# Up projection from the unscaled residual stream, with the norm's factor per token multiplied in by GpSimd

## The reference

```python
h = h + rmsnorm(mix, g_mix_post[i])
u = rmsnorm(h, g_ffn_pre[i])
up = causal_depthwise_conv(u @ w_up[i], conv_w[i], conv_b[i])
gate_ff, value = jnp.split(up, [D_FF], axis=-1)
f = (jax.nn.gelu(gate_ff, approximate=True) * value) @ w_down[i]
h = h + rmsnorm(f, g_ffn_post[i])
```

## Time and profile before

| | us |
|---|---|
| median of 3 runs | 3159.44 |
| lowest, highest | 3158.5, 3162.44 |
| profiled execution, its own time | 3159.64 |
| its span in the profile | 3157.8 |
| PE busy | 3089.1 |
| DVE busy | 1969.8 |
| ACT busy | 1419.3 |
| POOL busy | 35.0 |

### The profile page before, as it was taken

How to read it: one execution, slowest core, us unless ns; L and a number is a source line. 1 busy time by engine, 2 the same in 40 slices (tenths; PEclk the granted TensorE clock), 3 DMA queues, 4 the chain that set the end, 5 groups by cost and what they waited for, 6 DMA issues and landing times.

```text
span 3157.8 us, 41441 instructions
## 1 busy us (share of the span) xinstructions
PE 3089.1 (98%) x16976; PEld 2667.6 (84%) x16976; DVE 1969.8 (62%) x2503; ACT 1419.3 (45%) x2026; POOL 35.0 (1%) x30
## 2 busy tenths in 40 slices
PE   8999999989999999999999999999999999999998
PEld 8988887878888888878788888888889999899986
DVE  6767676788888878767867665342743444444444
ACT  5344555455555544436422222233644534544453
POOL 0000002000000000000000000000000000000000
PEclk9999999999999999999999999999999999999999
DMA  8777666756766778775555565343333333333343
GB/s 292 230 244 227 200 207 206 243 173 214 226 215 218 225 232 276 253 241 196 162 181 174 176 203 178 112 151 98 101 97 104 101 107 110 104 107 101 108 147 120
DMA packets 369837, 557.59 MB, mean 177 GB/s; under 512 B 16944, under 2 KB 239152, under 8 KB 368368
## 3 DMA queue, kind: packets, MB, share of 16 engines
q1 hardware_dynamic: 366784, 540.08, 53.4%
q0 software_dynamic: 2000, 12.06, 1.0%
q10 hardware_dynamic: 864, 2.80, 0.2%
HBM read 552.64 MB, written 2.23 MB: 176 GB/s over the span
## 4 chain that ended last, share of the span: by engine, by line
PE 91%; DVE 3%; ACT 2%; DMA 2%; issue 1%; SPq 0%; DVEq 0%; ACTq 0%
PE ps L708 87%; DVE wlo L1680 1%; DMA raw<-in_w_in 1%; ACT whi L1114 1%; PE ps L909 0%; PE ps L924 0%; PE ps L914 0%; PE ps L926 0%; DMA CX<-in_ctx 0%; DVE acc L1697 0%; PE ps L778 0%; PE ps L743 0%; DMA gb_c<-in_g_ffn_post 0%; DVE HCl L1834 0%; PE ps L837 0%
## 5 line engine op out<-in xcount | busy, mean ns | idle before, releaser
L1680 DVE TENSOR_TENSOR wlo<-raw,whi 128x1024 fp32r<-128x1024 f32 (+1 forms) x823 | 1002.1, 1223 | 827.6 <-ACT whi L1114 825.7
L1114 ACT ACTIVATE whi<-raw 128x1024 fp32r<-128x1024 f32 x828 | 868.1, 1056 | 1094.7 <-PE ps L708 1070.2
L708 PE MATMUL ps<-HCh,whi 128*128 128x512 f32 (+1 forms) x1816 | 508.1, 361 | 1.0 <-DVE HCl L1834 1.0
L708 PE MATMUL ps<-HCh,wlo 128*128 128x512 f32 (+1 forms) x1816 | 500.7, 357 | 0.0
L708 PE MATMUL ps<-HCl,whi 128*128 128x512 f32 (+1 forms) x1816 | 500.2, 357 | 0.0
L708 PE MATMUL ps<-V,whi 128*128 128x512 f32 x1408 | 444.1, 397 | 0.9 <-DVE V L1836 0.9
L1697 DVE SCALAR_TENSOR_TENSOR acc<-raw_ada,S,acc 128x1024 f32<-128x1024 f32 x330 | 420.8, 1285 | 8.1 <-DMA raw_ada<-in_ada_w 7.9
L708 PEld LDWEIGHTS ps<-HCl,whi 128*128 128x128 f32 x1816 | 323.5, 189 | 49.8
L708 PEld LDWEIGHTS ps<-HCh,wlo 128*128 128x128 f32 x1816 | 323.4, 189 | 49.9
L708 PEld LDWEIGHTS ps<-HCh,whi 128*128 128x128 f32 x1816 | 319.3, 189 | 51.0 <-issue 4.2
L708 PEld LDWEIGHTS ps<-V,wlo 128*128 128x128 f32 x1408 | 264.8, 188 | 62.6
(11 more groups left out here) (341 smaller groups left out, 3419.3 us busy)
## 6 DMA issues: line engine op xcount, KB each, us to landing
raw_ada<-in_ada_w SPq DMA_DIRECT2D x192, 512.0 KB, 4.8
raw<-in_w_up SPq DMA_DIRECT2D x176, 512.0 KB, 4.7
raw<-in_w_in SPq DMA_DIRECT2D x160, 512.0 KB, 3.9
raw<-in_od_w_in SPq DMA_DIRECT2D x160, 512.0 KB, 3.5
raw<-in_ev_w_in SPq DMA_DIRECT2D x96, 512.0 KB, 3.7
raw<-in_w_down SPq DMA_DIRECT2D x88, 512.0 KB, 5.1
raw<-in_w_out SPq DMA_DIRECT2D x32, 512.0 KB, 4.7
raw<-in_w_ple_gate SPq DMA_DIRECT2D x32, 512.0 KB, 4.5
```

The source lines that it names most:

```text
L708: mm = e.matmul(o, a, b, start=first and t == 0, stop=last, skip_group_check=True)
L1114: e.activation(m.whi[ch.i % SPLIT][:, 0:n], m.raw[ch.slot][:, 0:n], ACT.Copy).then_inc(S("hi"), 1)
L1680: e.tensor_tensor(m.wlo[ch.i % SPLIT][:, 0:n], m.raw[ch.slot][:, 0:n], m.whi[ch.i % SPLIT][:, 0:n].bitcast(F32), ALU.subtract).then_inc(S( ...
```

## The change

The up groups no longer take the normalized stream. V is made from `H` itself times `g_ffn_pre`, and PE turns `H` directly: `hnb` and line 1822 are gone for V. A column block is turned as soon as its two `residual` instructions are done. On DVE these alternate with the low parts of V. On ACT the eight squares no longer stand ahead of V; two of them follow each of the first four chunks' splits. The sum, the root and the inverse of norm `nb2` follow as steps beside `up1` and `up2`, then PE turns the factor into a row (`rsd2`, in the tenth chunk of the up stage), and DVE copies it to `rsb2` (128 x 256, the same row in every partition).

GpSimd multiplies `us` by `rsb2` after DVE's addition, 44 instructions of 128x512. ACT's first step of the convolution (line 1441 before, 1481 now) waits for `up_s`, the multiplication, in place of `set`, the addition. For groups 0, 1 and 2, whose factor isn't there in time, the step is put off by 7, 3 and 3 chunks on ACT and DVE (`LATE`). The load of gelu's table is put ahead of the first gelu.

```diff
+LATE = {0: 7, 1: 3, 2: 3}
...
-        self.V = Turned(self, "half", cut(V[:, 0, :, :]), cut(V[:, 1, :, :]), True,
-                        self.sb("hnb", [128, 2, 2, 512], F32, F + 104), None, lambda k: V[:, :, k, :])
+        self.V = Turned(self, "half", cut(V[:, 0, :, :]), cut(V[:, 1, :, :]), False, None, None,
+                        lambda k: V[:, :, k, :])
+        self.V.after = "b"
...
+    e.wait_ge(S("rsb2"), 1)
+    for n in range(2 * NUP):
+        G = plan.by[f"up{n}"]
+        e.wait_ge(S(f"set{G.s}"), G.freed)
+        us = m.us[n % 2]
+        e.tensor_tensor(us[:, :, :], us[:, :, :], m.rsb2[:, :].unsqueeze(1).to_broadcast([128, 2, T]),
+                        ALU.mult).then_inc(S("up_s"), 1)
     e.wait_ge(S("mm"), plan.by[f"up{2 * NUP - 1}"].done)
     e.dma_start(m.gb_c[:, :], A["g_ffn_post"].to_broadcast([128, D])).then_inc(S("ld_gb"), 16)
...
-                e.wait_ge(S("res"), 8 * RESIDUAL["c"] + 2 * (k // 4) + 2)
+                e.wait_ge(S("res"), 8 * RESIDUAL[X.after] + 2 * (k // 4) + 2)
...
-    for n in range(8):
-        P.again(m.nb2, "b", m.H, m.jb, n)
-    P.root(m.nb2)
     V = P.turned(m.V, lambda k: m.v("g_ffn_pre", k))
+
+    def factors():
+        for n in range(8):
+            P.again(m.nb2, "b", m.H, m.jb, n)
+            if n % 2:
+                yield
+        yield
+        yield
+        P.root(m.nb2)
+        P.gelu()
+        yield
+
+    P.beside.append(factors())
+    V.upto(0)
...
-        e.wait_ge(S(f"set{G.s}"), G.freed)
+        for _ in range(LATE.get(n, 0)):
+            yield
+        e.wait_ge(S("up_s"), n + 1)
...
-    residuals("b", m.Yw, m.H, m.nb.rs)
-    P.total(m.nb2)
-    P.invert(m.nb2)
-    V = P.turned(m.V, m.H, m.nb2.rs, lambda k: m.v("g_ffn_pre", k))
+    e.wait_ge(S("yg"), P.n_yg)
+    e.wait_ge(*P.freed)
+    V = P.turned(m.V, None, None, lambda k: m.v("g_ffn_pre", k))
+    for n in range(4):
+        P.residual("b", m.Yw, m.H, m.nb.rs, n)
+    V.upto(1)
+    for n in range(4, 8):
+        P.residual("b", m.Yw, m.H, m.nb.rs, n)
+        V.upto(n - 2)
+
+    def factors():
+        for _ in range(4):
+            yield
+        P.total(m.nb2)
+        yield
+        yield
+        yield
+        P.invert(m.nb2)
+        for b in range(2):
+            t = e.tensor_scalar(m.rsd2[:, b, :], m.ones[:, :], m.nb2.rs[:, b:b + 1], None, ALU.mult)
+        t.then_inc(S("rsd2"), 1)
+        yield
+        yield
+        e.wait_ge(S("rst2"), 1)
+        e.tensor_copy(m.rsb2[:, :], PS[4][:, 0:T]).then_inc(S("rsb2"), 1)
+        yield
```

More of the change, by code:

```diff
@@ L272, in __init__ @@
         self.third = third
+        self.after = "c"
         self.n_p, self.n_n = m.turns.get(row, (0, 0))
@@ L309, in __init__ @@
         at += 2.5
+        self.ji_at = at
         self.ji = self.sb("ji", [128, 2, 512], BF16, at)
@@ L373, in __init__ @@
         V = self.sb("V", [128, 2, NT, T], F32R, F)
-        self.V = Turned(self, "half", cut(V[:, 0, :, :]), cut(V[:, 1, :, :]), True,
-                        self.sb("hnb", [128, 2, 2, 512], F32, F + 104), None, lambda k: V[:, :, k, :])
+        self.V = Turned(self, "half", cut(V[:, 0, :, :]), cut(V[:, 1, :, :]), False, None, None,
+                        lambda k: V[:, :, k, :])
+        self.V.after = "b"
+        self.rsb2 = self.sb("rsb2", [128, T], F32, self.ji_at)
+        self.rsd2 = self.sb("rsd2", [128, 2, 128], F32, self.ji_at + 1)
         self.ACh, self.ACl = self.halves("AC", NF, T, F + 32)
@@ L996, in tensor @@
     X = P.turned(m.V)
+    def factors():
+        for _ in range(9):
+            yield
+        e.wait_ge(S("rsd2"), 1)
+        for b in range(2):
+            t = e.transpose(m.PS[4][:, 128 * b:128 * b + 128], m.rsd2[:, b, :], m.ident)
+        t.then_inc(S("rst2"), 1)
+        yield
+    P.beside.append(factors())
     for g in range(2 * NUP):
@@ L1120, in modulate, with gelu @@
             e.activation(m.R[l][:, :], m.PS[6 + l][:, :], ACT.Copy).then_inc(S("ada_R"), 1)
+    def gelu(self):
+        self.e.activation(self.m.SM[:, 24:25], self.m.ones[:, 0:1], ACT.Gelu_apprx_tanh)
     def warm(self):
```

## The result

| | us |
|---|---|
| changed kernel, median of 4 runs | 3189.12 (3187.57 to 3190.04) |
| kernel before, median of 4 runs on the same chip | 3160.94 (3158.5 to 3162.6) |
| ratio, 95% interval | 1.0087 (1.0074 to 1.0099) |
| span of the profiled execution, before and after | 3157.8 and 3187.9 |

The change makes the kernel 0.9% slower. Of the 30.1 us between the two spans, the timelines place all but a fraction. The first view is PE's timeline of the changed kernel, from the opening to the second stall; it answers to the earlier trace rows.

What follows compares the result with a forecast made beforehand. PE bounds the kernel, busy 3089.1 of 3157.8 us; the change makes DVE the bound in the up groups. Opening -5.3, link +28.7 and stage end +6.3 give +29.7 on 3159.44: 3189 us, range 3174 to 3205.

Steps and rivals of the forecast that it cites:

- The opening: Border of out3 and up0: first product 6.4 us earlier, 1.1 given back for squares, a gain of 5.3 us.
- The link: Up groups: GpSimd's multiplication, 1.25 us plus 0.11 for the step between engines, adds 1.36 us between addition and convolution.
- The bound: Up groups: DVE, with 0.66 us slack, becomes the bound; 0.70 us a group from group 3, 28.7 us lost.
- The period: Up stage: PE's time for a group, read as 11.11 us from 36 groups in a 400 us window.
- One sign: Up stage, changed kernel's trace: PE would have some 40 waits for wlo that sum to 28 us.
- The lock: SBUF exclusion between DVE and GpSimd: priced at nothing from group 3, at most 3.8 us for groups 0 to 2.
- The end of the stage: At down0: gb_c issued after up43's multiplication, 4.1 us more DVE wait plus 2.2 us lost lead, together 6.3 us.
- That the wait is hidden: Up stage: nothing starves, only the opening counts, 3158 us; both hidden cases together had chance 0.10.
- A slower GpSimd: Up stage: multiplication longer than half a wide row, 3204 us at 1.6 us, 3237 at 2.4; chance 0.08.

Runs made afterwards that it cites:

- e3: Changed kernel with ACT's first convolution step and DVE's taps one chunk later in groups 3 to 43 too; 3156.44 us, ratio 0.9990 to the kernel before.
- e1: Changed kernel without GpSimd's 44 multiplications, ACT waiting for DVE's addition again; 3155.71 us, ratio 0.9985 to the kernel before.
- e8: Kernel before with only GpSimd's multiplication (by ones) added between DVE's addition and ACT's first convolution step; 3195.08 us, ratio 1.0110.
- e2: Changed kernel with GpSimd multiplying 128x256 of the 128x512 elements, still one instruction a group; 3166.95 us, ratio 1.0020 to the kernel before.
- e4: Changed kernel with the multiplication done by DVE right behind its addition, GpSimd idle in the stage; 3163.46 us, ratio 1.0009 to the kernel before.
- e6: Kernel before with DVE's wait for gb_c put behind down0's splits; 3157.48 us, ratio 0.9994.
- e7: Changed kernel with steps one chunk later in all groups and the gb_c wait behind down0's splits; 3151.96 us, ratio 0.9975 to the kernel before.
- e5: Changed kernel with DVE's wait for gb_c put behind down0's splits; 3179.34 us, ratio 1.0059 to the kernel before.

## Why the prediction was right

The forecast was 3189; 3189.1 was measured. By its own steps:

- **The opening.** The first transposes were put at 643.3 and started at 643.42; the first product at 645.6, and it started at 645.70. 1.1 us were to be given back for the squares, and 1.4 were, which leaves 4.9 us for a forecast of 5.3. That the two are so close is luck. The squares cost their 0.35 us once, not three times; the other 1.0 us is PE's clock, granted at 0.53 instead of 0.78 in the first 4.3 us of products, for which the prediction had no term.
- **The link.** The multiplication was taken as 1.25 us from half of a wide row plus a fixed part; it takes 1.29 (half of 512 takes 0.737, so the fixed part is nearer 0.18 than 0.10). The link was put at 1.36 and is 1.37.
- **The bound.** DVE's wait was to be 2.59 and is 2.60; its waits for `whi` were to go, and went from 23.9 to 5.1. The loss was put at 28.7 and is 29.1 us. The period was read too short: the window of 400 us doesn't hold 36 whole groups, and from `up1` to `down0` a group took 11.20 us, not 11.11 (and then 11.88, not 11.79); this falls out of the difference. Two smaller errors cancel. PE first stood still five groups behind the start of `up1`, not from group 3 on, so the lead lasted longer; and behind it the loss was 0.74 us a group, not 0.70. One sign wasn't met as written: PE has 22 waits for `wlo` of 20.5 us, not some 40 of 28 us. Of the 29.1 us, 7.3 lie in what the profile counts as busy.
- **The lock.** It was priced at nothing in the changed kernel, since DVE stands still. e3 measured it where DVE doesn't: 0.83 us of DVE a group, against the 1.3 that I had written down for it. The Trainium skill, "SBUF — State Buffer", "Who interferes with whom", says that a DVE instruction with two SBUF inputs contends with a GpSimd instruction that reads SBUF. The trace agrees: the split beside POOL takes 2.32 us instead of 1.22. The prediction took from it that splits between the addition and the taps would lose 1.25 us a group in another way; in e3, which has this order, DVE loses 0.83 and PE nothing.
- **The end of the stage.** The term was 6.3 us and 6.1 were measured, but its parts were wrong. `gb_c` was to land 9.41 us after its issue, as before; it took 7.3. DVE waited 8.72 us, 2.0 more than before and not 4.1, and PE's stall was 5.73 us, 3.9 more than before, where the prediction had put all of its 6.3 there ("PE's wait at `down0` is about 8 us"). In return the prediction left out that PE's clock falls behind the stall, 2.2 us. The two errors cancelled, which is luck.
- **The rivals.** That the wait is hidden fell with e1 and e8. A slower GpSimd fell with the 44 rows, whose median is 1.29 us.

So the main step, a link of 1.37 us on a slack of about 0.6, was right and is shown by e1, e2, e3 and e8. That the total agrees to 0.1 us is luck: in the opening, the stage and its end alike, errors of about 1 to 2 us cancelled.

## What to carry to other kernels

Before a step is put between two engines "behind" the work, ask what the waiting engine has at the head of its queue meanwhile. If nothing, the step's full length is added to what that engine needs for a round, however idle the helper is, and it's free only as far as the engine's slack goes. Here the mean of the waits that end with PE's pace, 0.66 us a group, was a good guess of it: about 0.6 could be used. Count the first rounds by themselves. There the lead is small, and e4 lost most of its time in them. A repair is then a matter of order: one chunk's work moved into the wait made the same multiplication free here.

## What the runs showed of the hardware

- What a stall of PE costs beyond its length. The 444 products behind the wait at `down0` took 101.15 us after a stall of 1.87 us (before) and 101.16 after 2.04 (e4), at a granted clock of 1.00; 102.30 after 2.79 (e1), 102.55 after 2.73 (e3) and 102.59 after 4.34 (e2); 103.56 after 5.67 (e8) and 103.36 after 5.73 (the changed kernel, granted clock 0.51 for some 5 us). I had priced a stall by its length alone.
- GpSimd's end shows in the trace as others see it: ACT starts 0.03 us behind it. It took 0.737 us for 128x256 (two full operands, e2), 1.291 for 128x512 (one operand repeated) and 2.41 for 128x1024 (two full operands). These lie on one line, 0.18 us plus 2.2 ns an element of the row, so the repeated operand is no cheaper.
- A load of 1 MB spread to all partitions (`gb_c`) took 9.4 us to land before, and 9.9, 10.3 and 9.6 in e6, e1 and e4. Where POOL issued it behind its multiplication of `us` it took 6.8 to 8.1 (7.3 in the changed kernel and e8, 7.6 in e2, 7.9 in e3, 8.1 in e7, 6.8 in e5). It isn't PE's starving that makes it shorter, since PE never starved in the stage in e3 and e7. No run varied the moment of the issue alone, so the cause is open.
